# State-space scan of a hybrid block: its preparation set between the matmuls of the gate projection, its group norm spread over the scan and the first output tile

## The reference, cut to what matters

```python
z, xbc, dt_raw, ... = split(h @ w_in)
xbc = silu(causal_conv4(xbc, conv_w, conv_b))
xs, B, C = split(xbc)
dt = softplus(dt_raw + dt_bias);  A = -exp(a_log)
y = ssd(xs, dt, A, B, C, d_skip)     # per chunk: C B^T * decay, plus carried state
y = y * silu(z)
y = y * rsqrt(mean(y*y over each half of the features) + eps)
y_ssd = (y * ssd_norm_w) @ w_ssd_out          # later times sigmoid(gate)
```

## Time and profile before

| | us |
|---|---|
| median of 3 runs (2856.38 to 2858.42) | 2857.54 |
| span of the profiled execution | 2853.8 |
| PE busy in it | 2723.4 (95%) |
| DVE, ACT, POOL busy | 1551.6, 1225.6, 991.1 |
| chain that ended last, PE's share | 60% |

### The profile page before, as it was taken

The page is one execution under the profiler, slowest core; times in us unless marked ns, Lnnn a source line. Parts: engine busy times, 40 slices in busy tenths (PEclk is TensorE's granted clock), DMA queues, the critical chain, the costliest instruction groups (busy, mean ns, idle before and its releaser), DMA issues.

```text
span 2853.8 us, 39382 instructions
## 1 busy us (share of the span) xinstructions
PE 2723.4 (95%) x15752; PEld 2264.4 (79%) x15752; DVE 1551.6 (54%) x3031; ACT 1225.6 (43%) x2134; POOL 991.1 (35%) x729
## 2 busy tenths in 40 slices
PE   6989999999999999999999999999999999999997
PEld 4777878877878888878977788677898878788785
DVE  6668293071844977871358451255438228652683
ACT  4335245553224222242278463544443236553582
POOL 4611555403544444443323333200423420143422
PEclk8999999999999999999999999999999999999998
DMA  8312462202234555632200122100311230124102
GB/s 322 139 43 96 168 245 104 104 30 74 91 131 147 218 197 219 221 134 73 96 31 2 60 90 88 45 1 16 119 63 72 94 126 36 71 91 139 45 2 74
DMA packets 54293, 293.73 MB, mean 103 GB/s; under 512 B 4512, under 2 KB 8928, under 8 KB 24288
## 3 DMA queue, kind: packets, MB, share of 16 engines
q1 hardware_dynamic: 22464, 163.59, 16.1%
q10 hardware_dynamic: 31648, 127.63, 11.8%
HBM read 268.10 MB, written 17.86 MB: 100 GB/s over the span
## 4 chain that ended last, share of the span: by engine, by line
PE 60%; DVE 6%; ACT 3%; issue 2%; POOL 1%; DMA 0%; DVEq 0%; ACTq 0%; POOLq 0%
PE psum L478 15%; PE psum L480 15%; PE psum L479 15%; PE psum L1899 3%; PE psum L1946 2%; PE psum L1957 2%; PE psum L3945 2%; PE psum L1703 2%; PE psum L1726 2%; PE psum L1707 1%; PE psum L1715 1%; POOL w_lo L465 1%; DVE pair_row L1917 1%; DVE pair_prob L1926 1%; DVE c_decay L4063 1%
## 5 line engine op out<-in xcount | busy, mean ns | idle before, releaser
L465 POOL TENSOR_TENSOR w_lo<-raw,w_hi 128x512 fp32r<-128x512 f32 x612 | 853.8, 1426 | 1527.5 <-ACT w_hi L473 1527.4
L478 PE MATMUL psum<-a_hi,w_hi 128*128 128x512 f32 (+2 forms) x1880 | 703.5, 374 | 28.5 <-DVE a_lo L1091 16.2
L479 PE MATMUL psum<-a_lo,w_hi 128*128 128x512 f32 (+2 forms) x1880 | 688.6, 366 | 0.0
L480 PE MATMUL psum<-a_hi,w_lo 128*128 128x512 f32 (+2 forms) x1880 | 688.4, 366 | 0.0
L478 PEld LDWEIGHTS psum<-a_hi,w_hi 128*128 128x128 f32 (+1 forms) x1880 | 354.8, 189 | 102.4 <-issue 19.1
L479 PEld LDWEIGHTS psum<-a_lo,w_hi 128*128 128x128 f32 (+1 forms) x1880 | 355.0, 189 | 61.9 <-issue 5.1
L480 PEld LDWEIGHTS psum<-a_hi,w_lo 128*128 128x128 f32 (+1 forms) x1880 | 354.6, 189 | 59.3
L473 ACT ACTIVATE w_hi<-raw 128x2048 fp32r<-128x2048 f32 x153 | 292.4, 1911 | 170.6 <-DMA raw<-stream 137.5
L478 PE MATMUL psum<-w_hi,a_hi 128*128 128x256 f32 (+1 forms) x608 | 197.7, 325 | 1.8 <-POOL w_lo L465 1.6
L940 DVE SCALAR_TENSOR_TENSOR ada_temp<-ada_ring,psum 128x1024 f32<-128x1024 f32 x160 | 185.7, 1216 | 17.4 <-ACT psum L1063 14.0
L480 PE MATMUL psum<-w_hi,a_lo 128*128 128x256 f32 (+1 forms) x608 | 193.1, 318 | 0.0
(11 more groups left out here) (479 smaller groups left out, 4735.4 us busy)
## 6 DMA issues: line engine op xcount, KB each, us to landing
raw<-stream SPq DMA_DIRECT2D x153, 1024.0 KB, 4.8
ada_ring<-ada ACTq DMA_DIRECT2D x72, 1024.0 KB, 6.0
x_in<-xres ACTq DMA_DIRECT2D x3, 3072.0 KB, 10.8
xres<-x_in ACTq DMA_DIRECT2D x3, 2048.0 KB, 6.9
partner<-gq ACTq DMA_DIRECT2D x4, 1024.0 KB, 9.5
xres<-x_in ACTq DMA_DIRECT2D x1, 3072.0 KB, 11.1
own_raw<-stream SPq DMA_DIRECT2D x3, 1024.0 KB, 4.8
xres<-x_in ACTq DMA_DIRECT2D x3, 1024.0 KB, 4.8
```

Of the source, the lines that this page charges most:

```text
L465: last = pool.tensor_tensor(k.lo_of(s)[:, cols], k.raw_of(s)[:, cols], k.hi_of(s)[:, cols].bitcast(F32), ALU.subtract)
L478: pe.matmul(out, lhs[0], rhs[0], start=start, stop=False)
L479: pe.matmul(out, lhs[0], rhs[1], start=False, stop=False)
L480: return pe.matmul(out, lhs[1], rhs[0], start=False, stop=stop)
```

## The change

`slot_plan` orders xbc, dt, z. `ssd_branch` runs xbc first (with `lead=2`, a filler ahead of step 4 only, no modulation), then dt, then z on four banks with a `ScanSteps` side: four transposes of dt (tile 0, step 6), the step sizes, two sum matmuls (tile 2, step 0), transposes (38, those of B's last chunk are left out), state sums, products of B and C and the first two decay rows stand between steps of z's tiles; all barriers from xbc to the scan's end are gone. The scan itself is as before on other banks; squares of finished features follow every second head on ScalarE, sums of them on PE from head 7 on, the rest (`ScanNorm`) in tile 0 of `gated`, where also roots, scaling, the high part of y (now on ScalarE) and its low part stand. `gated` carries all 16 slots (8 to 23), two in its first tile and one in each of the next fourteen.

```diff
-    slots("z", "w_in", full, R(z0, 1024))
-    slots("dt", "w_in", full, R(dt0, 16))
     slots("xbc", "w_in", full, R(xbc0, 1536))
+    slots("dt", "w_in", full, R(dt0, 16))
+    slots("z", "w_in", full, R(z0, 1024))
...
+class ScanSteps(Side):
+    TURN_AT = {(2 + n // 3, (1, 4, 7)[n % 3]): n for n in range(11)}
+    STATE_AT = {(3, 5): 0, (4, 5): 1, (5, 5): 2}
+    CB_AT = {(6, 1): 0, (6, 2): 1}
+    ROWS_AT = {(7, 5): 0, (7, 6): 1}
...
+    def within(self, pe, t, j):
+        if at == (2, 0):
+            pe.wait_ge(self.to_pe.sem, self.to_pe.at(1))
...
+class ScanNorm(Side):
...
+    def within(self, pe, t, j):
+        if t == 0 and j in (1, 2, 4):
+            self.add_up(pe, {1: 5, 2: 6, 4: 7}[j])
+
+    def early_scalar(self, act, t):
+        k = self.k
+        if t:
+            return
+        for g in range(2):
+            act.wait_ge(self.summed.sem, self.summed.at(4 * g + 4))
+            k.act_chain(act, act.activation(self.rstd[:, g], self.bank(g), ACT.Ln, bias=k.eps[:], scale=1.0 / 512))
+        for g in range(2):
+            act.activation(self.rstd[:, g], self.rstd[:, g], ACT.Exp, scale=-0.5).then_inc(self.rooted.sem, 1)
+        for f in range(8):
+            act.wait_ge(self.scaled.sem, self.scaled.at(f + 1))
+            act.activation(self.y[0][:, f, :], self.z[:, f, :], ACT.Copy).then_inc(self.high.sem, 1)
...
+        for f in range(8):
+            if f % 4 == 0:
+                dve.wait_ge(self.rooted.sem, self.rooted.at(f // 4 + 1))
+            dve.scalar_tensor_tensor(self.z[:, f, :], self.z[:, f, :], k.col("ssd_norm_w", f), self.rstd[:, f // 4],
+                                     ALU.mult, ALU.mult).then_inc(self.scaled.sem, 1)
+            if f:
+                low(f - 1)
+        low(7)
...
-    dense(k, block, ["z"], feature_major(a, KC, full), ada=ada.of(8), barrier=False, lead=2, lead_fill={4: 4, 6: 14},
-          act_tile=lambda act, i, t, ps: act.activation(z[:, t, :], ps, ACT.Silu))
...
-    dense(k, block, ["xbc"], feature_major(a, KC, full),
+    dense(k, block, ["xbc"], feature_major(a, KC, full), barrier=False, lead=2, lead_fill={4: 4},
...
+    dense(k, block, ["z"], feature_major(a, KC, full), barrier=False, n_banks=4,
+          rest_free=k.tile_free.at(-2), side=steps,
+          act_tile=lambda act, i, t, ps: act.activation(z[:, t, :], ps, ACT.Silu))
...
+            if h >= 5 and h % 2:
+                norm.square(act, (h - 5) // 2, y_used)
+        act.preload_act_table_set("natural_log")
+        norm.square(act, 6, y_used)
+        norm.square(act, 7, y_used)
...
+        pe.wait_ge(k.tile_free.sem, z_taken)
         for h in range(SSD_HEADS):
             f, off = h // 2, 64 * (h % 2)
             if h + 2 < SSD_HEADS:
-                rows(h + 2)
+                pe.wait_ge(dec_ready.sem, dec_ready.at(h + 1))
+                steps.decay_rows(pe, h + 2)
...
+            if h >= 7 and h % 2:
+                norm.add_up(pe, (h - 7) // 2)
...
-          rhs_ready=y_ready, ada=k.ada.group(8, B0 + 49152, B0 + 86016, B0 + 81920, 3, new_rows=True).of(8))
+          rhs_ready={(f, 2): norm.ready(f) for f in range(8)}, side=norm,
+          ada=k.ada.group(16, B0 + 49152, B0 + 86016, B0 + 81920, 3, new_rows=True).of(16))
```

More of the change, by code:

```diff
@@ L75, in slot_plan @@
     k0, v0, u0, g0 = q0 + 1536, q0 + 3072, q0 + 4608, q0 + 5632
+    slots("xbc", "w_in", full, R(xbc0, 1536))
+    slots("dt", "w_in", full, R(dt0, 16))
     slots("z", "w_in", full, R(z0, 1024))
-    slots("dt", "w_in", full, R(dt0, 16))
-    slots("xbc", "w_in", full, R(xbc0, 1536))
     for c in range(4):
@@ new lines, with __init__, square, add_up @@
+class ScanNorm(Side):
+    def __init__(self, k, z, y, squares, rstd):
+        self.k, self.z, self.y, self.squares, self.rstd = k, z, y, squares, rstd
+        self.squared, self.summed, self.rooted, self.scaled, self.high, self.low = (
+            k.sem_named(f"ssd_norm_{x}") for x in ("squared", "summed", "rooted", "scaled", "high", "low"))
+        self.bank = lambda g: k.psum[:, g, :]
+    def square(self, act, f, used):
+        act.wait_ge(used.sem, used.at(f + 1))
+        if f >= 4:
+            act.wait_ge(self.summed.sem, self.summed.at(f - 3))
+        act.activation(self.squares[:, f % 4], self.z[:, f, :], ACT.Square).then_inc(self.squared.sem, 1)
+    def add_up(self, pe, f):
+        pe.wait_ge(self.squared.sem, self.squared.at(f + 1))
+        pe.matmul(self.bank(f // 4), self.k.cst("ones"), self.squares[:, f % 4], start=f % 4 == 0, stop=f % 4 == 3) \
+            .then_inc(self.summed.sem, 1)
+    def within(self, pe, t, j):
+        if t == 0 and j in (1, 2, 4):
+            self.add_up(pe, {1: 5, 2: 6, 4: 7}[j])
+    def early_scalar(self, act, t):
+        k = self.k
+        if t:
+            return
+        for g in range(2):
+            act.wait_ge(self.summed.sem, self.summed.at(4 * g + 4))
+            k.act_chain(act, act.activation(self.rstd[:, g], self.bank(g), ACT.Ln, bias=k.eps[:], scale=1.0 / 512))
+        for g in range(2):
+            act.activation(self.rstd[:, g], self.rstd[:, g], ACT.Exp, scale=-0.5).then_inc(self.rooted.sem, 1)
+        for f in range(8):
+            act.wait_ge(self.scaled.sem, self.scaled.at(f + 1))
+            act.activation(self.y[0][:, f, :], self.z[:, f, :], ACT.Copy).then_inc(self.high.sem, 1)
+    def on_vector(self, dve, t):
+        k = self.k
+        if t:
+            return
+        def low(f):
+            dve.wait_ge(self.high.sem, self.high.at(f + 1))
+            dve.tensor_tensor(self.y[1][:, f, :], self.z[:, f, :], self.y[0][:, f, :].bitcast(F32), ALU.subtract) \
+                .then_inc(self.low.sem, 1)
+        for f in range(8):
[6 more added lines that the diff above has]
+        low(7)
+    def ready(self, f):
+        return self.low.sem, self.low.at(f + 1)
+    def over(self):
+        for s_, n in ((self.squared, 8), (self.summed, 8), (self.rooted, 2), (self.scaled, 8), (self.high, 8),
+                      (self.low, 8)):
+            s_.stage_over(n)
@@ L1130, in ssd_branch @@
     full = [(0, S)]
-    ada = k.ada.group(8, B0 + 40960, k.ARENA + 32768 + 8192, k.ARENA + 32768, 3)
-    dense(k, block, ["z"], feature_major(a, KC, full), ada=ada.of(8), barrier=False, lead=2, lead_fill={4: 4, 6: 14},
-          act_tile=lambda act, i, t, ps: act.activation(z[:, t, :], ps, ACT.Silu))
[L1136 to L1139, removed]
+    dt_rows = k.at("dt_rows", k.ARENA + 36864, [16, S])
     pad = k.at("pad", small, [P, 4, S + 3])
@@ L1169, in ssd_branch @@
[L1169 to L1299, removed]
-                last = pe.matmul(k.psum[:, 2 * c + g, :], b_tok[:, c, g * P:(g + 1) * P],
-                                 xd[:, c % 2, g * 512:(g + 1) * 512], start=True, stop=True)
-            last.then_inc(summed.sem, 1)
-        for g in range(2):
-            for c in range(4):
-                last = pe.matmul(k.psum[:, 6 + g, c * P:(c + 1) * P], xbc[:, 8 + g, c * P:(c + 1) * P],
-                                 xbc[:, 10 + g, c * P:(c + 1) * P], start=True, stop=True)
@@ L1309, in ssd_branch @@
[L1309 to L1314, removed]
-    o = small + 2560
-    seg = k.at("seg", o + 4096, [P, 3, 512])
-    ea = k.at("ea", o + 10240, [P, 3, 512])
+          act_last=lambda act, i, t: act.activation(xbc[:, t, :], conv[:, t % 2], ACT.Silu))
+    other_constants_in(k, block)
+    dense(k, block, ["dt"], few_rows(a, 16, full), barrier=False,
+          act_tile=lambda act, i, t, ps: act.activation(dt_rows[:], ps[0:16, :], ACT.Copy))
@@ new lines, in ssd_branch @@
+    steps = ScanSteps(k, (x_tok, b_tok, h_prev, xbc, small), dt_rows)
+    dense(k, block, ["z"], feature_major(a, KC, full), barrier=False, n_banks=4,
+          rest_free=k.tile_free.at(-2), side=steps,
+          act_tile=lambda act, i, t, ps: act.activation(z[:, t, :], ps, ACT.Silu))
+    steps.over()
+    z_taken = k.tile_free.at(0)
+    acum, nacum, cb = steps.acum, steps.nacum, steps.cb
+    c4 = steps.c4
+    norm = ScanNorm(k, z, (k.at("y_hi", B0 + 16384, [P, 8, S], F32R), k.at("y_lo", B0 + 32768, [P, 8, S], F32R)),
+                    k.at("squares", B0 + 98304, [P, 4, S]), k.at("rstd", B0 + 73728, [P, 2, S]))
@@ L1370, in _ @@
                 act.activation(decay, decay, ACT.Exp, bias=c4(nacum)[:, c, h:h + 1])
-            act.activation(ea[:, h % 3], k.psum[:, h % 2, :], ACT.Exp).then_inc(dec_ready.sem, 1)
+            act.activation(ea[:, h % 3], k.psum[:, 4 + h % 2, :], ACT.Exp).then_inc(dec_ready.sem, 1)
+            if h >= 5 and h % 2:
[3 more added lines that the diff above has]
+        norm.square(act, 7, y_used)
     @block.tensor
     def _(pe):
-        def rows(h):
-            if h >= 2:
-                pe.wait_ge(dec_ready.sem, dec_ready.at(h - 1))
-            for c in range(4):
-                last = pe.matmul(k.psum[:, h % 2, c * P:(c + 1) * P], c4(da)[:, c, h:h + 1].broadcast_to([P, P]),
-                                 k.cst("tri"), start=True, stop=True)
-            last.then_inc(rows_out.sem, 1)
```

(10 more changed lines are left out.)

223 lines of the change are left out of this document (181 added, 42 removed).

## The result

The changed kernel takes 2834.07 us (median of 4 runs, 2831.17 to 2835.53), beside 2857.69 for the kernel before (4 runs): a ratio of 0.9915, with a 95% interval of 0.9901 to 0.9929, so 23.6 us less. The forecast was 2834.9. The stage table is made of this pair.

The account below looks back on a forecast made before the run. PE, busy 95% of the span, was taken as the bound. Terms of -5.85, -22.3, +5.3 and +0.2 summed to -22.6 us, from a median of 2857.5 to 2834.9, with an 8-in-10 range of 2822 to 2847.

Parts of the forecast that it names:

- Preparation beside z: From last xbc tile to head 2's decay rows: 40.82 us shrink to 14.6 on PE plus 3.9 idle, -22.3 us.
- the rival of steps that wait for each other: In z: PE waits about 1 us at ten of 18 places, giving 2845 us; chance 0.12.
- First tiles: First two tiles: the filler ahead of step 6 goes and no wait replaces it, -5.85 us.
- Scan: Head 2's decay rows to last head: four sums cost 3.4 us, half-rate clock 1.9, together +5.3 us.
- the slower rival: Scan starts cold and its short matmuls never bring the clock back, giving 2876 us; chance 0.04.
- Norm and output: Last head to end of `gated`: the norm's 15 us return as waits, 102.8 against 102.6, +0.2 us.
- The rival of the hidden norm: Output stage: tiles 4 and 6 don't wait, gain 32 to 33, giving 2825 us; chance 0.20.
- the starving rival: Output tiles 8 to 15 take 6.7 instead of 5.44 us, +10, giving 2845 us; chance 0.12.
- Table switch: ScalarE's table load costs 1.28 us; rival adds a drain at each of five switches, giving 2842 us; chance 0.01.
- Products beside low parts: Output stage: a VectorE product takes 1.14 us alone, 2.24 beside GpSimd; GpSimd's low part 5.04 alone, 8.03 beside products.

Follow-up runs that it names:

- e7_first_warm: Changed kernel with 12 instead of 4 filler calls ahead of step 4 of the first two tiles: 2832.02 us, ratio 0.9903 to the kernel before.
- e1_filler_back: Changed kernel with the old filler ahead of step 6 of the first two tiles put back: 2840.82 us, ratio 0.9938 to the kernel before.
- e3_norm_serial: Changed kernel with the norm put back as a serial stage between scan and `gated`: 2834.48 us, ratio 0.9915 to the kernel before.
- e5_products_later: Changed kernel with modulation products and loads of `gated` started at its tile 3: 2824.81 us, ratio 0.9881 to the kernel before.
- e4_refills_early: Changed kernel with ScalarE's refills for output tiles 4 and 6 moved earlier, products unmoved: 2827.17 us, ratio 0.9893 to the kernel before.
- e9_products_later_warm: Changed kernel with `gated` products from tile 3, nine fillers ahead of the scan, twelve ahead of step 4 of the first tiles: 2822.89 us, ratio 0.9872.

## Why the prediction was right

The time was met within 1 us, and by the forecast's own mechanisms, but not each term by its size. That it is so close is in part luck: the pair of profiles gives 20.1 for the 22.6, with 3.7 missing in the first tiles and 1.2 too much in the other four rows, and the medians lie 3.5 us further apart than this pair.

- **Preparation beside z: right.** PE multiplies weights unbroken from 48.35 to z. z runs from 116.71 to 175.37 = 58.66 us; less 192 matmuls at 0.2265 (43.5) and the one wait of 0.30, the side work took 14.9, forecast 14.6. So, within 0.3 us over all of them, short matmuls among weight matmuls cost what they cost alone in the earlier trace rows; they don't hide. The gap ahead of the scan is 3.85, forecast 3.9. VectorE never held PE for more than 0.30, so the rival of steps that wait for each other falls.
- **First tiles: the term was mis-sized in this profile, -2.1 for -5.85.** The forecast took the stretch before step 4 as given, and PE's own rows differ there: before, it idled 2.06 us ahead of step 4 and kept the clock; after, step 4 came 1.1 us later (48.35 for 47.23, both released by `a_lo`, which the change doesn't touch) behind 4.74 us of idle time, and ran at half rate until about 54.5. The same 24 matmuls took 8.4 us for 5.8, so 1.1 + 2.6 is the 3.7 that is missing. The clock's part is shown by `e7_first_warm` (2.8 there). The 1.1 stands already at the first weight matmul of this stage (31.36 for 30.23, which waits for `a_lo` too), and the profiles of all kernels here have this row between 30.23 and 31.59. By medians, `e1_filler_back` gives the filler 6.75 us. That the same two things make up the 3.5 us between the pair of profiles (20.1) and the medians (23.6) is likely and not shown.
- **Scan: right, +4.7 for +5.3**, the clock 2.2 for 1.9 and the sums 2.5 for 3.4, which the forecast added in full although PE had 1.15 us of idle time for them. The clock was back by 184, 5 us behind the first row, so the slower rival falls.
- **Norm and output: right, and for the reason given.** The forecast said that the norm's time would come back as waits of 4.0 and about 2 ahead of tiles 4 and 6, tile 6 at S + 46.5; the rows have 3.56 and 2.23, tile 6 at S + 45.6, each with a low stretch of the clock behind. y's own waits were smaller (0.30 twice, forecast 2.1). `e3_norm_serial` shows that spreading the norm gained nothing, `e5_products_later` that the gain is there (6 to 8 us) once the products are out of the way. The rival of the hidden norm failed on both things that the forecast named: on ScalarE's strict order, since `e4_refills_early` takes both waits away by order alone, and on the products beside GpSimd, since the first wait falls from 3.56 to 1.68 when the low part runs alone. Low parts after tile 8 are in time: from 284 to 329 PE is busy 45.00 of 45 us with 16 slots in flight, so the starving rival falls too.
- **Table switch.** ScalarE's load is 1.28 us and the activation behind it starts 0.02 later (235.20 and 236.50), as before, and the logarithm ahead of the load ends at 235.19. The Trainium skill (ScalarE: Activation LUTs, What ACT_TABLE_LOAD costs) adds 1380 ns of drain to each; the row does not show it, and the chain's end at S + 30.5 leaves no room for it.
- **Products beside low parts.** A product takes 2.27 while GpSimd works and 1.21 after it ended at 257.77, and the first low part takes 6.95 beside products instead of 5.04. The Trainium skill (SBUF — State Buffer, section SBUF: two separate sides) describes an exclusive lock between the two engines for a whole instruction, where VectorE's has two inputs in SBUF as here; the rows agree.

## What to carry to other kernels

A stage that is taken off the path by hanging it into the next one doesn't vanish: add up the in-order queue of each engine that the next stage's weights need, from the last instruction of the old stage to the first weight that comes out, and compare it with the moment PE wants it. Here that sum gave both waits to within half a microsecond, and it also names the cure: background work (modulation products and loads) starts only when the critical refills are through. Fillers are worth keeping where PE waits anyway and work that PE bounds follows, and pure loss where nothing is waited for. Which of the two one has is seen in the row of idle time behind them, and in the waits that appear later when they are taken out.

## What the runs showed that was not expected

- The same idle time can be followed by either clock. Idle of 2.31 at 404.34 after the change was followed by a clock of 1.00; idle of 2.32 at 390.76 in `e9_products_later_warm`, the same place of the program, by 0.57. These are the stretches of 4 us from each:

```profile
404.00:408.00 4.00, 3.66 (x16) 3.05 (x17) 4.00 (x5) 0.00 (x0) 4.00 (x3) 1.00 0.30 125
```

```profile
390.70:394.70 4.00, 3.94 (x10) 3.12 (x11) 4.00 (x6) 0.28 (x1) 4.00 (x3) 0.57 0.24 102
```

  Likewise idle time of 2.51 at 350.07 after the change gave 0.68 and at 341.02 in `e4_refills_early` 1.00, and in the first tiles 3.16 gave 0.65 in `e1_filler_back`, while 3.12 in `e5_products_later` gave 1.00. A row of idle time thus costs its length or some 2 us more, and a few such rows in one execution can move its time by several us. What decides it stays open.
- Background load has a place as well as an amount: the same 16 slots with the same bytes cost 6 to 8 us less in this stage when they began three tiles later.
